# Hybrid attention and mixture-of-experts decoder: weights in 19 slots of 1 MiB with a map of period two, released per pass, and further rounds in an inner loop

## What is computed

```python
for l in range(DEPTH):                       # DEPTH = 2
    proj = rms_norm(x, norm1_g[l]) @ w_in[l]                       # 1024 x 3072
    x = x + concat([diff_attention(...), stick_breaking(...)]) @ w_out[l]   # 1024 x 1024
    h2 = rms_norm(x, norm2_g[l])
    # router: best of 4 groups, then the best 2 of its 8 experts, weights "combine"
    hg = einsum('sd,edf->sef', h2, w_gate)   # 32 experts, 1024 x 256 each
    hu = einsum('sd,edf->sef', h2, w_up)
    x = x + einsum('sef,efd->sd', silu(hg) * hu * combine, w_down)
```

## Time and profile before

| what | value |
|---|---|
| runs | 848.56, 855.61, 856.1 us, median 855.61 us |
| span of the profiled execution | 850.2 us, 10581 instructions |
| mean granted clock of TensorE | 0.940 of full speed |
| PE busy | 687.0 us (81%) |
| HBM read | 238.54 MB |
| packets on q8, PE's instruction queue | 74 |
| activations (L764): 8 sets in 2 layers, and second rounds | 18 |

### The profile page before, as it was taken

The page is one execution under the profiler, slowest core; times in us unless marked ns, Lnnn a source line. Parts: engine busy times, 40 slices in busy tenths (PEclk is TensorE's granted clock), DMA queues, the critical chain, the costliest instruction groups (busy, mean ns, idle before and its releaser), DMA issues.

```text
span 850.2 us, 10581 instructions
## 1 busy us (share of the span) xinstructions
PE 687.0 (81%) x3752; PEld 341.8 (40%) x3753; DVE 310.9 (37%) x692; ACT 123.8 (15%) x302; POOL 9.0 (1%) x19
## 2 busy tenths in 40 slices
PE   7998999887487487787799989997874874777885
PEld 4445464553133133252344445647331331332423
DVE  0437622543223223333325363425332331333333
ACT  3115421200000000000031343211000000000100
POOL 0000000010000000000020000000000000000000
PEclk9998999999889799899999999998987997998999
DMA  8894046759999999957297220492599999999441
GB/s 288 275 391 161 1 180 269 292 116 383 417 419 402 419 398 420 420 228 310 90 356 285 100 99 24 182 422 115 190 423 417 373 422 418 387 422 420 183 167 52
DMA packets 49815, 240.93 MB, mean 283 GB/s; under 512 B 7424, under 2 KB 7712, under 8 KB 25152
## 3 DMA queue, kind: packets, MB, share of 16 engines
q1 hardware_dynamic: 49120, 238.61, 70.4%
q0 software_dynamic: 608, 0.99, 1.0%
HBM read 238.54 MB, written 1.05 MB: 282 GB/s over the span
## 4 chain that ended last, share of the span: by engine, by line
PE 66%; issue 17%; PEldq 5%; DVE 4%; ACT 2%; PEld 2%; DVEq 1%; DMA 1%; ACTq 1%; SPq 0%
PE bank L1014 18%; PE bank L1159 17%; PE bank L1140 9%; PE bank L1185 7%; PE bank L1112 6%; PEldq L1178 4%; PE bank L1071 1%; ACT qkT L533 1%; PE bank L1058 1%; PEld bank L1176 1%; PE bank L1176 1%; DMA wbuf<-in_w_in 1%; PE bank L1091 1%; PE bank L1034 1%; PEldq L1323 1%
## 5 line engine op out<-in xcount | busy, mean ns | idle before, releaser
L1159 PE MATMUL bank<-wbuf,qkT 128*32 128x512 f32 x1024 | 137.7, 686 | 80.8 <-issue 79.6
L1014 PE MATMUL bank<-wbuf,hTbuf 128*128 128x512 f32 x384 | 170.1, 600 | 2.5 <-DMA wbuf<-in_w_in 2.0
L1159 PEld LDWEIGHTS bank<-wbuf,qkT 128*32 128x32 f32 x1024 | 39.1, 124 | 176.9 <-issue 175.3
L1014 PEld LDWEIGHTS bank<-wbuf,hTbuf 128*128 128x128 f32 x384 | 72.5, 192 | 90.8 <-issue 88.5
L1140 PE MATMUL bank<-qkT,xn 128*128 128x128 f32 x576 | 70.1, 281 | 20.2 <-issue 20.2
L1140 PEld LDWEIGHTS bank<-qkT,xn 128*128 128x128 f32 x576 | 67.0, 195 | 34.7 <-issue 34.6
L787 DVE TENSOR_TENSOR x_sb<-x_sb,bank 128x512 f32<-128x512 f32 x72 | 46.2, 684 | 77.2 <-PE bank L1185 77.2
L1176 PE MATMUL bank<-dnbuf,qkT 128*32 128x512 f32 x512 | 61.6, 597 | 11.4 <-DVE qkT L776 7.7
L764 DVE TENSOR_SCALAR qkT<-qkT 128x256 f32<-128x256 f32 x18 | 5.3, 294 | 156.4 <-ACT qkT L529 156.4
L1112 PE MATMUL bank<-wbuf,hTbuf 128*128 128x512 f32 x128 | 56.0, 593 | 0.0
L529 ACT ACTIVATE qkT<-bank 128x256 f32<-128x256 f32 x18 | 6.9, 384 | 287.5 <-PEq L1162 287.5
(11 more groups left out here) (187 smaller groups left out, 580.9 us busy)
## 6 DMA issues: line engine op xcount, KB each, us to landing
wbuf<-in_w_gate SPq DMA_DIRECT2D x64, 1024.0 KB, 12.5
wbuf<-in_w_up SPq DMA_DIRECT2D x64, 1024.0 KB, 16.8
dnbuf<-in_w_down SPq DMA_DIRECT2D x56, 1024.0 KB, 10.7
wbuf<-in_w_in SPq DMA_DIRECT2D x10, 2048.0 KB, 18.4
wbuf<-in_w_out SPq DMA_DIRECT2D x4, 2048.0 KB, 18.0
wbuf<-in_w_down SPq DMA_DIRECT2D x8, 1024.0 KB, 12.2
wbuf<-in_w_in SPq DMA_DIRECT2D x4, 1024.0 KB, 8.5
x_sb<-in_x SPq DMA_DIRECT2D x2, 512.0 KB, 4.1
```

Of the source, the lines that this page charges most:

```text
L1014: last = MM(ps[PROJ_BANK[i][t]][:, :], hT[:, k, t * P:(t + 1) * P], w[:, k, :], start=(k == 0), stop=(k == KC - 1))
L1159: MM(ps[2][j * SLOTS:(j + 1) * SLOTS, :].rearrange("p (a f) -> p a f", a=2), src[:, k, j * SLOTS:(j + 1) * SLOTS], halves[:, gate:up + 1:u ...
```

## The change

1. `wbuf` becomes 19 slots of 1 MiB, `dnbuf` goes. Tables give each matrix its slot; gate and up of even and odd sets have their own, but for up 3 (slot 9) in both; the four down slots serve all sets. The projection blocks take two slots each.
2. SP's expert loads are written out for all sets. The order per set is new: when `gate_up` of set g-1 is done (`gu_used`), up 3 of set g and the four gates of set g+1 (5 MiB); when its `down` is done (`dn_used`), the four downs of set g and up 0 to 2 of set g+1 (7 MiB). Both semaphores are raised once, in the last round that a set needs.
3. The loads of the next layer's projections no longer wait for the whole last set.
4. PE has one loop of four pairs. The woven second round goes: rounds 2 to 8 stand in one inner loop of seven turns behind the first round, entered only if a set needs a second round. A turn that isn't needed raises the owed semaphores.
5. DVE copies the activations (`act_copy`) behind the gathered tokens and weights (`gather_copy`), not ahead of them. PE reads the token count ahead of `gate_up`. The PSUM banks of the activation transposes and of the later rounds are others.

```diff
-        wbuf = sb("wbuf", [P, (SLOTS_W + 1) * SLOT + SLOT // 2])
-        dnbuf = sb("dnbuf", [P, LANES, FC * D])
+        wbuf = sb("wbuf", [P, SLOTS_W * SLOT])
...
+GATE_SLOT = [[0, 1, 2, 3], [17, 18, 15, 12]]
+UP_SLOT = [[4, 5, SLOT_STAGE, 9], [6, 7, 8, 9]]
+DOWN_SLOT = [10, 11, SLOT_VALUES, 16]
...
-        def further_rounds(eng, n_set, most, late, whole, owed):
+        def further_rounds(eng, n_set, most, whole, owed):
+
             base = eng.snap(n_set * MORE)
             with eng.If(most > SLOTS):
...
+                with eng.Fori(1, ROUNDS) as r:
+                    with eng.If(most > r * SLOTS):
+                        whole(eng.snap(base + r), r)
+                    with eng.Else():
+                        eng.drain()
+                        for s in owed:
+                            eng.sem_inc(s, 1)
+                eng.drain()
...
+            def load_further_sets(l):
+                for g in range(1, SETS):
+                    if g > 1:
+                        for j in range(LANES - 1):
+                            load_up(l, g, j)
+                    sp_.wait_ge(gu_used, l * SETS + g)
+                    load_up(l, g, LANES - 1)
+                    if g + 1 < SETS:
+                        for j in range(LANES):
+                            load_gate(l, g + 1, j)
+                    sp_.wait_ge(dn_used, l * SETS + g)
                     for j in range(LANES):
...
+                        load_down(l, g, j)
+
+            def load_next_layer(l):
+                for i in range(3):
+                    load_block(l, i)
+                sp_.wait_ge(gu_used, l * SETS)
+                load_block(l, 3)
+                load_block(l, 4)
+                sp_.wait_ge(dn_used, l * SETS)
+                load_block(l, 5)
+                load_half(l, IN_BLOCKS, 0)
...
-                activate(first, n)
-                act_copy(first, n)
-                gather_copy(first, dve.snap(g + l * GATHERS + 2), hgT, selwT2[1 - parity], 6)
...
+                activate(first, n, FIRST_GU)
+                gather_copy(first, dve.snap(g + l * GATHERS + 2), hgT, selwT2[1 - parity], first_half)
+                act_copy(first, n, first_half)
                 y_copy(first, n)
...
+                def whole(m, r):
+                    pe.wait_ge(x_more, m)
                     pe.wait_ge(first["hg_d"], g + (l * GATHERS + 2))
                     pe.wait_ge(first["hg_a"], g + (l * GATHERS + 2))
                     gather(more, m, sel_more)
...
+                    transpose_weights(more, m, more_half, selw_more)
+                    gate_up(more, m, MORE_GU, hgT_more, parity)
+                    with pe.If(most <= r * SLOTS + SLOTS):
+                        pe.sem_inc(gu_used, 1)
+                    transpose_act(more, m, more_half)
+                    down(more, m)
+                    with pe.If(most <= r * SLOTS + SLOTS):
                         pe.sem_inc(dn_used, 1)
...
-                with pe.Fori(0, SETS // 2 - 1) as pair:
-                    expert_set(l, pe.snap(pair * 2), 0, False)
-                    expert_set(l, pe.snap(pair * 2 + 1), 1, False)
-                with pe.Fori(SETS // 2 - 1, SETS // 2) as pair:
-                    expert_set(l, pe.snap(pair * 2), 0, False)
-                    expert_set(l, pe.snap(pair * 2 + 1), 1, True)
+                with pe.Fori(0, SETS // 2) as pair:
+                    for parity in range(2):
+                        expert_set(l, pair, parity)
```

More of the change, by code:

```diff
@@ L525, in gather_copy, with gate @@
                 nc.scalar.copy(dst[:, 4:8, :], ps[1][:, :].rearrange("p (k s) -> p k s", k=4)).then_inc(s["hg_a"], 1)
-            def gate(s, n):
+            def gate(s, n, bank):
                 act.wait_ge(s["gu_ps"], n)
-                nc.scalar.activation(eg, ps[2][:, 0:FF], ACT.Exp, scale=-1.0).then_inc(s["gate_exp"], 1)
+                nc.scalar.activation(eg, ps[bank][:, 0:FF], ACT.Exp, scale=-1.0).then_inc(s["gate_exp"], 1)
             def y_copy(s, n):
@@ L533, in y_copy, with expert_set @@
                 nc.scalar.copy(y[:, HALF:], ps[5][:, :]).then_inc(s["y_a"], 1)
-            def early(n):
-                gather_copy(more, n, hgT_more)
-                gate(more, n)
-            def late(n):
-                y_copy(more, n)
-            def whole(n, r):
-                early(n)
-                late(n)
+            def whole(m, r):
+                gather_copy(more, m, hgT_more)
+                gate(more, m, MORE_GU)
+                y_copy(more, m)
+            def expert_set(l, g):
+                most = act.value_load(cnt[0:1, bass.ds(g, 1)], min_val=0, max_val=SEQ)
+                n = act.snap(g + l * SETS + 1)
+                gate(first, n, FIRST_GU)
+                gather_copy(first, act.snap(g + l * GATHERS + 2), hgT)
+                y_copy(first, n)
+                further_rounds(act, g + l * SETS, most, whole, ACT_MORE)
             for l in range(DEPTH):
@@ L609, in _ @@
                 with act.Fori(0, SETS) as g:
-                    most = act.value_load(cnt[0:1, bass.ds(g, 1)], min_val=0, max_val=SEQ)
-                    gate(first, act.snap(g + l * SETS + 1))
-                    gather_copy(first, act.snap(g + l * GATHERS + 2), hgT)
-                    second_round_early(act, g + l * SETS, most, early)
-                    y_copy(first, act.snap(g + l * SETS + 1))
-                    further_rounds(act, g + l * SETS, most, late, whole, ACT_MORE)
+                    expert_set(l, g)
         @block.vector
@@ L786, in into_x @@
                         c = slice(h * HALF, (h + 1) * HALF)
-                        last = V.tensor_tensor(x_sb[:, t, c], x_sb[:, t, c], ps[SC_BANK[t][h]][:, :], ALU.add)
-                    if t == 0 and s is first:
-                        last.then_inc(x_moe0, 1)
+                        V.tensor_tensor(x_sb[:, t, c], x_sb[:, t, c], ps[SC_BANK[t][h]][:, :], ALU.add)
                 gap().then_inc(done, 1)
@@ L1208, in early @@
                     gather(more, m, sel_more)
-                    transpose_weights(more, m, 7, selw_more)
-                    gate_up(more, m, hgT_more, l, parity)
-                    pe.wait_ge(more["selwT_out"], m)
-                    with pe.If(most <= 2 * SLOTS):
-                        pe.sem_inc(slot_used, LANES)
-                def late(m):
-                    pe.wait_ge(more["actT_out"], m)
-                    pe.wait_ge(x_moe0, n)
-                    down(more, l, last)
-                    with pe.If(most <= 2 * SLOTS):
-                        pe.sem_inc(dn_used, 1)
-                    pe.wait_ge(x_moe, g + (l * SETS + 2))
-                    scatter(more, m, selwT_more)
@@ new lines, in expert_set @@
+                with pe.If(most <= SLOTS):
+                    pe.sem_inc(gu_used, 1)
+                following = pe.snap(g + (l * GATHERS + 2))
+                gather(first, following)
+                pe.wait_ge(x_moe, n)
+                pe.wait_ge(x_more, g * MORE + (l * SETS * MORE + 1))
+                pe.wait_ge(first["selwT_out"], g + (l * GATHERS + 1))
+                transpose_weights(first, following, first_half)
+                transpose_act(first, n, first_half)
+                for j in range(LANES):
+                    pe.wait_ge(dn_in[j], g * 16 + (l * SETS + 1) * 16)
@@ L1243, in expert_set @@
+                down(first, n)
                 with pe.If(most <= SLOTS):
                     pe.sem_inc(dn_used, 1)
-                with pe.If(most > SLOTS):
-                    transpose_act(more, pe.snap(g * MORE + (l * SETS * MORE + 1)))
-                pe.wait_ge(first["selwT_out"], g + (l * GATHERS + 2))
+                pe.wait_ge(first["selwT_out"], following)
                 scatter(first, n, selwT2[parity])
-                further_rounds(pe, g + l * SETS, most, late, whole, PE_MORE)
@@ L1250, in expert_set @@
-                with pe.If(most > 2 * SLOTS):
-                    pe.sem_inc(slot_used, LANES)
-                    pe.sem_inc(dn_used, 1)
+                further_rounds(pe, g + l * SETS, most, whole, PE_MORE)
             x_chunked = x_sb[:, :, :].rearrange("p t (c k) -> p t k c", k=KC)
```

315 lines of the change are left out of this document (126 added, 189 removed).

## The result

The changed kernel takes 882.38 us (median of four runs, 880.17 to 884.34) against 855.06 us of the kernel before: a ratio of 1.034, with a 95% interval of 1.028 to 1.040. It is slower, by about 27 us. Single executions of the kernel before took 842 to 857 us over all comparisons, and the ratios leave out those more than 1.5% above its fastest, so a ratio can differ from the quotient of two medians. The profiled execution has a span of 881.4 us and a device time of 883.16 us; 890.8 us was forecast.

A forecast was written before the change was run, and what follows sets the result against it. The prediction took PE to bound attention and, in the expert stage, DMA together with PE's instruction-fetch stalls. Its terms gave +18.5 and +16.7 us, together +35.2 on 855.6: 890.8 us, range 868 to 925.

The forecast's parts named there:

- Term A: Expert stage to the end of set 6's first scatter: earlier with DMA as the bound, -5.5 and -9 us.
- Term B: Set 6's second round: run alone as a chain, 30.9 us against 21.2 woven, +9.7 us per layer.
- Term C: Between set 6's scatter and set 7's gate/up: six unneeded loop turns, nothing hides them, +12.6 us per layer.
- Term D: Set 7: slower gate/up after PE's idle time and a later `act_copy`, +1.7 and +3.4 us.
- attention stage: Stage ahead of the experts: PE bounds it, so the change costs and gives nothing there.
- Code that is kept: PE's pair loop: about 6 packets instead of 9, taken as no longer fetched; branch back well under 1 us.
- rival 1: PE's pair loop is still fetched in each turn, PE bounds the expert stage as now: 920 us, chance 0.15.
- second rival: PE's small inner loop is also fetched each turn, seven branches back at 6.1 us per layer: 1006 us, chance 0.06.
- Memory: The on-chip weight store: 19 MiB before and after, so no gain is due to more room.
- Rival 3: Not slower: PE reaches the tail early and turns are cheap, repaying the serial round; 861 us, chance 0.07.

The follow-up runs named there:

- e3_before_short: The kernel before with the code for rounds 3 to 8 left out on PE alone: 827.20 us, ratio 0.976 to the kernel before.
- e4_pad74: The changed kernel with 74 never-run matmuls added to each set's PE code, behind a jump, pair loop 1839 instructions: 964.75 us, ratio 1.137 to the kernel before.
- e11_act_first: The changed kernel without the six unneeded turns and with the activations copied ahead of the gathered tokens again: 858.26 us, ratio 1.014 to the kernel before.
- e7_map_short: The changed kernel's memory map and loads with the woven rounds and code layout of before, rounds 3 to 8 left out on PE: 826.86 us.
- e10_after: The changed kernel run again, unchanged: 878.84 us, ratio 1.039 to the kernel before.
- e6_pad60: The changed kernel with 60 never-run matmuls added to each set's PE code, pair loop 1727 instructions: 907.80 us, ratio 1.063 to the kernel before.
- e8_map_only: The kernel before with all its rounds, but the changed kernel's memory map and loads and one loop over four pairs: median 871.66 us, no interval.
- e9_aligned: The kernel of e6_pad60 with each layer's pair loop started on a border of the 256-instruction blocks: 892.24 us, ratio 1.051 to the kernel before.
- e12_misaligned: The kernel of e9_aligned with each layer's pair loop started 100 instructions behind a block border: 931.18 us, ratio 1.098 to the kernel before.

## Why the prediction was right, by its steps

The forecast of a slower kernel held, and its cause: a gain from code that is kept, outweighed by a serial second round and empty turns. 882.4 us lie 8.4 below the 890.8. Of these, 4.0 are in the span, 881.4 us against 885.4. The other 4.4 come from the 5.4 us that I added between span and median: here the median is 1.0 us above the span. Measured between the same events in the two traces (for A, the event of before is the one that the prediction works out, 375.1 us, and by the same steps 797.9 in the second layer):

| term | forecast, first / second layer | measured |
|---|---|---|
| A, end of set 6's first scatter | -5.5 / -9 | -5.6 / -11.7 |
| B, to the end of the second | +9.7 / +9.7 | +10.4 / +11.7 |
| C, to set 7's gate/up | +12.6 / +12.6 | +10.0 / +10.4 |
| D, set 7 | +1.7 / +3.4 | +0.5 / +2.3 |
| attention stage | 0 / 0 | +3.7 / +0.4 |
| end of the first layer | 0 | -1.0 |

So the closeness is in part luck: the four terms came 7 us lower than forecast, and 4 us of attention stage, which has nothing to do with the change, made up for half of it.

**Code that is kept.** Right, with the evidence named: L1264 at 0.2 us and 19 packets, where 25 were forecast. e3_before_short and e4_pad74 show it as the cause from both sides. That the removed copy would do it was open in the prediction (0.15 for rival 1); 1245 instructions are well under the border. The second rival, the small inner loop fetched each turn, is excluded by its own branch back, L294, at 0.21 us. The Trainium skill ("Runtime: NRT & Kernel Launch", section "Instruction fetch mechanics") would have a fetch at each taken branch out of a window of two pages, and this trace does not agree: the pair loop, 1245 instructions in 5 or 6 blocks, branches back in 0.2 us.

**Term A.** First layer right: 373.2 us against 369.5 absolute, of which the attention stage gave 3.65. DMA had no break from 190 us on. In the second layer it gained 2.7 us more than forecast: the step took the stream's length as the same in both, and there the scatter ended 191.7 us behind set 0's gate/up instead of 193.8.

**Term B.** Its value was 0.7 and 2.0 us low. The parts, in the first layer: waits of 3.48 and 3.87 us, and gather (5.44) and down (5.55) slower than 3.83 and 3.95, both behind such a wait. The slower work is 3.2 us, and I allowed 1.7 for the clock. The term compares with the woven round of before, behind whose fetches set 6's down weights had long landed. With the code kept in both, the full price of the serial round is 14.5 and 14.1 us a layer (61.5 and 61.2 in e11_act_first against 47.0 and 47.1 in e7_map_short), since the woven round then also fills a wait for the down weights.

**Term C** is the mis-sized one, by 2.6 and 2.2 us. The working took 2.1 us a turn and charged all six in full. A turn takes 1.92 us. What the six add to the boundary of before is less, (12.72 - 2.75) / 6 = 1.66 us each and 1.74 in the second layer, since one set of increments, some 1.1 us, stood in that boundary already (behind the second round, in one go), and the first turn's branches pass while PE still works on the scatter. e11_act_first confirms the whole at 20.6 us for both layers.

**Term D and the attention stage.** Set 7 had the 9.4 and 9.8 us gate/up as forecast. The later `act_copy` costs 0.5 us once a layer, and taking it back gained nothing. The first attention stage was 3.65 us longer, which I had at 0. It is not the change: with the same code in that stage, set 0 starts at 175.25 us in e10_after and 173.01 in e6_pad60, and at 179.4 in the trace of the changed kernel. It is how executions differ.

**Memory.** Right, with the code kept: the map is worth nothing, shown by e7_map_short against e3_before_short. For a loop that is fetched again, e8_map_only leaves it open.

**The rivals.** Rival 1 did not happen. Its price of 920 us left out that the first set's jump over the further rounds stalls too; e4_pad74, the nearest run, took 965, but with stalls of 47 us at a jump that rival 1's kernel does not have, so whether 920 was far off is not shown. Rival 3 asked for a turn under 1 us; it is 1.9.

Where did the time go? By the medians beside each other, keeping PE's code gains 22 to 27 us (e3_before_short, e7_map_short; 20 and 25 by the ratios), the serial round gives back 31 (858.26 - 826.86, from different comparisons; 28.6 in the traces), and the empty turns 20.6.

## What to carry to other kernels

A loop that fits the instruction store is worth more than its instruction count says: measure it by the packets on the engine's own instruction queue and by the duration of the branch back, and keep rarely run paths short or out of the loop, since never-run code, with the jump over it, cost 82 us here. A second pass that is woven in costs less where the first waits for weights (here some 17 to 19 us instead of 32 or 33), and making it serial to save code pays only if no other way is found to save it; here a shared inner loop, or one prefetch hint, was. Empty turns of a hardware loop are work on the path: end the loop at the count that is needed and pay the semaphores at once.

## What the runs showed that I had not expected

- **A border in blocks, not in instructions.** q8's packets are 16 KB (1.21 MB in 74), and I count them as blocks of 256 instructions. The first layer's loop starts four instructions ahead of a block border. Counted without these four, every loop of 5 to 7 blocks was kept and every one of 8 lost, unless hinted. Leaving them out is an assumption that no run tests: strictly counted, the first layer's loop of e6_pad60 touches 8 blocks and was kept. The clean pair is e9_aligned and e12_misaligned, in both layers: 1727 instructions in 7 blocks had a branch back of 0.208 us, in 8 blocks one of 6.07 us.
- This would agree with the Trainium skill's 128 KiB for PE, refilled in blocks of 16 KiB or 256 instructions ("Runtime: NRT & Kernel Launch", section "Instruction fetch mechanics"), eight blocks, if one of them is always being filled ahead. That is my reading and was not shown by itself.
- **The hint changes what is kept.** With it, 8 blocks were kept and q8 fell from 74 to 38 packets. That the hint takes the place of the block fetched ahead would explain it; no run tests this.
- **A miss took 6 us under load and less without.** While the weights came at 420 GB/s it took mostly 5.5 to 6.5 us, in some places up to 7.8; behind the last set of the second layer, when nothing is left to load, 2.9 to 4.8. Some misses in the middle were shorter too, such as the 3 to 4 us of before, so the load need not be the whole reason. Jumps over 241 to 413 instructions missed like branches back over 1839.
